# A decoder layer with 32 routed experts on one core: the second stream's experts in another order

## The reference

```python
logits = (h @ w_router + b_router)                  # 512 tokens x 32 experts
top_val, top_exp = lax.top_k(logits, 4)             # four experts for each token
gate_w = softmax(top_val)
# for each expert e, on the tokens that chose it:
gt = minimum(x @ w_gate[e] + b_gate[e], 7.0)
up = clip(x @ w_up[e] + b_up[e], -7.0, 7.0)
y  = (gt * sigmoid(1.702 * gt) * (up + 1.0)) @ w_down[e] + b_down[e]
# the four y of a token are summed with their gate_w, then residual and layer norm
```

## Time and profile before

| | us |
|---|---|
| median of 3 runs (lowest, highest) | 1703.16 (1700.87, 1704.95) |
| profiled execution | 1702.35 |
| its span, first to last instruction | 1700.4 |
| PE busy | 1450.3 |
| PE, line 1057, idle before it | 151.1 |
| DVE busy | 716.5 |
| mean granted TensorE clock | 0.900 |

### The profile page before, as it was taken

How to read it: one execution, slowest core, us unless ns; L and a number is a source line. 1 busy time by engine, 2 the same in 40 slices (tenths; PEclk the granted TensorE clock), 3 DMA queues, 4 the chain that set the end, 5 groups by cost and what they waited for, 6 DMA issues and landing times. The chain is left out here.

```text
span 1700.4 us, 38833 instructions
## 1 busy us (share of the span) xinstructions
PE 1450.3 (85%) x13689; PEld 566.2 (33%) x13690; DVE 716.5 (42%) x2483; ACT 203.4 (12%) x525; POOL 294.0 (17%) x220
## 2 busy tenths in 40 slices
PE   6999988889839875787797997997999997979783
PEld 3444445445413321222232332332333332323221
DVE  1138775555944331233242443342444442424234
ACT  1011255550010000000000000000000000000002
POOL 0010000123512110111111221121122221212111
PEclk8999979989859986899897998997999997979786
DMA  9721156923474999999998899879979879495993
GB/s 347 197 75 50 37 178 233 288 82 128 147 317 149 405 409 409 409 409 404 408 357 320 318 346 402 305 271 407 403 291 373 318 264 362 139 407 202 405 408 121
DMA packets 162520, 488.93 MB, mean 288 GB/s; under 512 B 40375, under 2 KB 59891, under 8 KB 145076
## 3 DMA queue, kind: packets, MB, share of 16 engines
q1 hardware_dynamic: 146356, 471.63, 71.4%
q0 software_dynamic: 16128, 16.82, 4.9%
HBM read 474.60 MB, written 17.96 MB: 290 GB/s over the span
## 5 line engine op out<-in xcount | busy, mean ns | idle before, releaser
L1057 PE MATMUL banks<-arena,master 128*32 128x512 f32 x5248 | 674.8, 636 | 151.1 <-DMA arena<-in_w_up 141.0
L1072 PE MATMUL banks<-arena,master 128*32 128x256 f32 x5248 | 346.1, 394 | 6.0 <-DVE master L1769 4.5
L1726 DVE STREAM_TRANSPOSE master<-master 128x256 f32<-128x256 f32 x83 | 54.1, 652 | 672.3 <-PE banks L1057 653.6
L1057 PEld LDWEIGHTS banks<-arena,master 128*32 128x32 f32 x5248 | 152.8, 112 | 504.0 <-DMA arena<-in_w_up 250.4
L660 POOL DMA_INDIRECT master<-moe_input,misc x84 | 93.3, 1111 | 882.3 <-DVE misc L1757 836.3
L1072 PEld LDWEIGHTS banks<-arena,master 128*32 128x32 f32 x5248 | 158.3, 113 | 153.3 <-issue 70.4
L1305 ACT ACTIVATE master<-master 128x256 f32<-128x256 f32 x82 | 34.2, 417 | 1118.7 <-DVE master L1791 1118.7
L676 POOL DMA_INDIRECT moe_output<-master,misc x82 | 130.2, 1587 | 103.0 <-issue 96.8
L1737 DVE TENSOR_SCALAR master<-cbias 128x128 bf16<-128x128 f32 x340 | 95.4, 344 | 44.7 <-issue 44.0
L825 PE MATMUL banks<-arena 128*128 128x512 f32 x256 | 112.6, 595 | 0.0
L1480 DVE CUSTOM_DVE_ANT_0 arena<-banks,master 128x128 f32<-128x128 f32 (+3 forms) x96 | 46.0, 480 | 64.4 <-PE banks L913 63.9
(11 more groups left out here) (307 smaller groups left out, 1128.5 us busy)
## 6 DMA issues: line engine op xcount, KB each, us to landing
arena<-in_w_gate SPq DMA_DIRECT2D x256, 512.0 KB, 13.8
arena<-in_w_up SPq DMA_DIRECT2D x256, 512.0 KB, 14.8
arena<-in_w_down SPq DMA_DIRECT2D x128, 1024.0 KB, 15.4
arena<-in_w_ada SPq DMA_DIRECT2D x12, 2048.0 KB, 13.1
arena<-in_x SPq DMA_DIRECT2D x2, 2048.0 KB, 8.3
arena<-in_w_in SPq DMA_DIRECT2D x2, 2048.0 KB, 9.7
master<-bias_by_distance SPq DMA_DIRECT2D x16, 256.0 KB, 4.5
arena<-in_w_in SPq DMA_DIRECT2D x8, 256.0 KB, 4.2
```

Source lines behind the costliest of these rows:

```text
L1057: last = nc.tensor.matmul(two(bank[0][strip(j), :]), hTe[:, k, :], arena[:, 24 * b + 2 * k:24 * b + 2 * k + 2, quarter(j)], start=(k == 0) ...
L1072: last = nc.tensor.matmul(bank[1][strip(j), 0:256], actT[:, q, c, :], DN(b, q, c)[:, quarter(j)], start=(q == 0 and c == 0), stop=(q == 3 ...
L1726: nc.vector.transpose(hTe, xg.rearrange("p (t k) -> p k t", k=KC)).then_inc(s_xe, 1)
```

## The change

The diff:

```diff
             (rank, cum, total, inA1, sumA, gap, fill, inA, turn, second, place, nA, before, rest, start, pos, nB, pairs, ending,
-             shift) = ccol[0:20]
+             many, wide, count, late_half, over) = ccol[0:24]
...
             row_of(inA1, tA)
+            nc.vector.tensor_reduce(many, tA, AX.X, ALU.add)
             total_where(tA, sumA)
...
             link(nc.vector.tensor_tensor(inA, inA1, fill, ALU.max))
-            nc.vector.tensor_scalar(turn, rank, -2.0, 128.0, ALU.mult, ALU.add)
+            nc.vector.tensor_tensor(wide, rank, gap, ALU.add)
+            link(nc.vector.tensor_tensor(count, many, gap, ALU.add))
+            link(nc.vector.scalar_tensor_tensor(late_half, wide, 2.0, count, ALU.mult, ALU.subtract))
+            nc.vector.scalar_tensor_tensor(turn, wide, -2.0, rank, ALU.mult, ALU.subtract)
+            nc.vector.tensor_scalar(over, count, -30.5, None, ALU.add)
+            link(nc.vector.tensor_scalar(late_half, late_half, 29.0, None, ALU.is_le))
+            link(nc.vector.scalar_tensor_tensor(turn, late_half, over, turn, ALU.mult, ALU.add))
+            nc.vector.tensor_scalar(turn, turn, 188.0, None, ALU.add)
             link(nc.vector.tensor_scalar(second, inA, -1.0, 1.0, ALU.mult, ALU.add))
             link(nc.vector.scalar_tensor_tensor(place, turn, second, rank, ALU.mult, ALU.add))
```

## The result

The changed kernel takes 1717.2 us (median of 4 runs, 1715.81 to 1720.44), against 1702.35 us of the kernel before (4 runs, one more than in the table before, 1700.87 to 1704.95). The ratio is 1.0088, with a 95% interval of 1.0068 to 1.0108: slower by 14.9 us. The profiled execution took 1720.44 us, 3.2 us above the median, so stall sums from its trace are a little high.

The account below looks back on a forecast made before the run. PE and the DMA engines limit in turn in the expert stage. The order's +12.1 us and the tables' 1.0 us on 1702.35 give 1715.5; with the median 0.8 us higher, 1716 us was predicted, range 1710 to 1723.

Parts of the forecast that it names:

- The law: Expert stage, items 5 to 81: stalls follow from distances in items between neighbouring expert starts; 224.1 us become 236.2.
- lone distances of two: Two expert starts two items apart, with more room around: 7.2 us each, four places, 28.8 us.
- one and two together: Starts one and two items apart in succession, at 10/11/13 and 43/45/46: 27.5 us each, 55.0 together.
- couples: Two expert starts one item apart, alone, at 63/64 and 72/73: 18.15 us each, 36.3 together.
- triples: Three expert starts in a row, at 23/24/25, 35/36/37 and 78/79/80: 38.15 us each, together 114.5.
- the small waits for DVE: Two short waits for DVE in the expert stage, 1.20 and 0.44 us before, taken as kept.
- The step that decided the sign: Pricing three starts in a row at 38.15 us each; below 33.8 us each the change would be faster.
- the point left open: Whether a distance of three is quite free after 7, behind stalled 5/7: between 0 and 2 us, taken as 0.
- The front: Up to item 23 the run of ones is gone: stalls of 104.4 us become 41.9, a gain of 62 us.
- The tables: DVE's nine new instructions, less one, ahead of item 0's first matmul: +1.0 us, bounds 0.6 and 1.5.
- The mechanism as I worded it: SP's in-order queue waits for one expert's down slots, so the next load starts only about when that expert is computed.
- The rule on interleaving regimes: Whole kernel: one with several regimes may gain from interleaving them, so this change makes it faster; no size given.

Follow-up runs that it names:

- the kernel without triples: Changed kernel with three neighbours of stream B exchanged via a table by rank, so no three starts lie in a row; 1685.22 us, ratio to before 0.9895.
- the spread order: Changed kernel with stream B in an order picked by the distance law for these inputs, from a table by rank; 1617.22 us, ratio to before 0.9495.
- the control: Changed kernel with SP's loop over the experts written out with constants, loads in the same order; 1709.19 us, ratio to before 1.0033.
- the written-out list: SP's loop over the experts unrolled with constants: 1709.19 us against the changed kernel's 1717.2, and 1610.76 us against the spread order's 1617.22.

## Why the prediction was right

I predicted 1716 us; 1717.2 was measured, and the likeliest case came. That the two lie within 1.2 us is in part luck: the profiled execution, which the sum of 1715.5 is to be held against, took 1720.44, and the terms below miss in both directions.

- *The law.* Predicted for the changed order 236.2 us of stalls, 239.3 found in an execution that was itself 3 us slow. By kind: lone distances of two +2.0, one and two together +2.0, couples +1.3, triples -1.3, and the small waits for DVE -0.9, since the one at item 40 did not come again.
- *Triples*, 38.15 each: 882.82 - 811.11 - 34.4 = 37.3 for the first, 1670.82 - 1598.97 - 34.4 = 37.5 for the last, and 38.4 for the one between. The step that decided the sign held, and without the triples the kernel became faster than before.
- *Distances of one and two together*, 27.5: 10/11/13 took 700.27 - 625.16 - 45.8 = 29.3. It was at the upper end of its bounds; 43/45/46 cost 27.7. Whether the distance of three ahead of 10 kept some of the slack, the point left open, stays open: the same starts cost 27.6 in the kernel without triples.
- *Lone distances of two*, 7.2: 602.24 - 583.45 - 11.46 = 7.3 for the first, 7.7 as the mean of the four; the spread order shows 8.0 as the mean of eight. Mis-sized by 0.5 to 0.8, since it rested on one row.
- *Couples*, 18.15: 72/73 took 1553.13 - 1510.45 - 22.9 = 19.8, and 63/64 17.9. 72/73 lies behind a distance of three too, but so it does without triples, where it cost 18.3.
- *The front*: item 23 was 57.5 us earlier, of 62 predicted, since item 5 itself started 2.5 us later, and the mis-sized terms made up the other 2. For the same two reasons item 53 was 1.7 us earlier, of 6 predicted, and item 81 17.8 us later, for 13.
- *The tables*, 1.0: 1.1 in the trace.
- *The mechanism as I worded it* was wrong in part. I read from the earlier trace rows that SP's queue holds the next load back and took that for the cause. It does hold it back, but freeing it moved the wait from one item to the next. And of the 7.2 us in the earlier trace rows from the down loads at 876.33 to 883.55, the last 3.7 are no wait for a slot at all but the head of SP's loop, as the last section shows. The prices came from rows and so did not depend on it; a remedy built on that wording would have disappointed.
- *The rule on interleaving regimes* (the Trainium skill, "Perfetto Trace Analysis", section "Optimization Strategy"): the trace agrees with it for the spread order, whose DMA share is 0.95 to 1.02 throughout and which gained 84 us, and disagrees for the changed order, which interleaved sizes and lost 15. What has to be spread is the starts of loads, over both streams together.

## What to carry to other kernels

Where two streams share one load path, and each has a single slot, list the starts of both on one axis and price the distances: a load that takes 32 us against items of 11.46 us wants three items between starts, whichever stream they are in. Rearranging one stream by its own sizes, blind to where the other one changes, moves the stalls and may add to them. A wait seen behind a queue is not yet caused by it: give the queue a head start and see whether the sum falls.

## What the runs showed that I had not expected

DMAs whose addresses and waits come from registers cost SP more time. Between the last down load of one expert and the first loads of the next, SP's loop reads four numbers from the tables. In the changed kernel, around the experts that start at items 23 and 24, this is the row of SP:

```profile
807.32 3.55 SPq L455 DMA_DIRECT2D arena<-in_w_down  x4
814.58 0.37 SPq L461 DMA_DIRECT2D misc<-bias_parts  x1
815.25 0.35 SPq L449 DMA_DIRECT2D arena<-in_w_gate  x1
815.81 0.34 SPq L449 DMA_DIRECT2D arena<-in_w_up  x1
```

With constants, in the control:

```profile
807.48 3.73 SPq L455 DMA_DIRECT2D arena<-in_w_down  x4
811.31 0.35 SPq L461 DMA_DIRECT2D misc<-bias_parts  x1
811.71 0.33 SPq L449 DMA_DIRECT2D arena<-in_w_gate  x1
812.09 0.43 SPq L449 DMA_DIRECT2D arena<-in_w_up  x1
```

The bias load and the first gate and up loads go out 0.67 and 0.56 us apart with registers, 0.40 and 0.38 with constants. The gap ahead of them is larger: 3.7 us against 0.1. In the changed kernel it is never under 3.5 us, and it is 3.5 to 3.8 at the 16 places where the next start is one or two items away; in the control it is 0.1 or 1.9 us there. So with registers the first parts of a load come later than the slot would allow, in a stage where PE waits for just these. At each lone distance of two the written-out list brings the stall from 7.7 to 6.7 us on average in the changed order, and from 8.0 to 7.0 in the spread one; the 31.9 us of the item in the middle of a triple stay. Over the stage the stalls fall by 11.2 us in the changed order and by 11.8 in the spread one. How much of this is the head of the loop and how much the pace of issue was not tried apart.
